# A hybrid decoder step on one Trainium2 core: two stages of a hand-written order change places

## What is computed

```python
h = _rmsnorm(x, g_norm1) * (1.0 + scale1) + shift1
z = h @ w_in                      # q|k|v|gates of both mixers
qk = jax.nn.silu(conv_b + sum(xpad[:, j:j + T] * conv_w[j] for j in range(4)))   # mixer A (mLSTM): 4-tap convolution of q and k
ha = _head_norm(_mlstm(...)) * jax.nn.sigmoid(o_a)
la = jax.nn.log_sigmoid(lr_b @ w_alpha + b_alpha) / 16                            # mixer B (GLA): log decay per channel and token
hb = _head_norm(_gla(qb, kb, vb, la, S0)) * jax.nn.silu(r_b)
y = (jax.nn.sigmoid(g_a) * ha + jax.nn.sigmoid(g_b) * hb) @ w_out
x = x + gate1 * y
x = x + gate2 * (silu(h2 @ w_ffn_gate) * (h2 @ w_ffn_up)) @ w_ffn_down
```

## Time and profile before

| | before |
|---|---|
| median of three runs | 1924.56 us |
| the profiled execution | 1924.94 us |
| its span, first to last instruction | 1923.1 us |
| PE (TensorE) busy | 98% |
| VectorE / ScalarE / GpSimd busy | 55% / 37% / 36% (DVE / ACT / POOL) |
| mean granted TensorE clock | 0.992 of full speed |

### The profile page before, as it was taken

One profiled execution on the slowest core, in us unless ns is written; L12 is line 12 of the kernel. 1 busy time (PEld: TensorE's weight loads), 2 busy tenths in 40 slices (PEclk: granted clock), 3 DMA queues, 4 the chain that ended last, 5 costly groups with the idle time before them and its releaser, 6 DMA issues.

```text
span 1923.1 us, 33344 instructions
## 1 busy us (share of the span) xinstructions
PE 1884.8 (98%) x13211; PEld 1805.1 (94%) x13211; DVE 1066.3 (55%) x1875; ACT 701.5 (36%) x1449; POOL 706.9 (37%) x600
## 2 busy tenths in 40 slices
PE   7899999999999999999999999999999999999998
PEld 4899999999999999999998899999999999999998
DVE  5740654414553236524174679886756675666566
ACT  4533434334233243342343554322232223222327
POOL 3221332212232213313132585433454345434544
PEclk8999999999999999999999999999999999999999
DMA  9241221332222322214233553111121112111212
GB/s 338 75 101 50 75 81 53 107 84 69 81 58 70 105 80 72 59 58 130 54 87 112 189 148 95 44 34 55 45 67 36 54 45 66 39 51 45 67 40 96
DMA packets 212226, 154.62 MB, mean 80 GB/s; under 512 B 11252, under 2 KB 196788, under 8 KB 211560
## 3 DMA queue, kind: packets, MB, share of 16 engines
q1 hardware_dynamic: 211770, 152.27, 26.7%
q10 hardware_dynamic: 302, 0.22, 0.0%
HBM read 130.96 MB, written 21.50 MB: 79 GB/s over the span
## 4 chain that ended last, share of the span: by engine, by line
PE 85%; DVE 7%; issue 2%; POOL 2%; ACT 2%; DMA 1%; SPq 0%; ACTq 0%; DVEq 0%; POOLq 0%
PE bank L923 36%; PE bank L2134 19%; PE bank L2103 12%; PE bank L1011 3%; PE bank L2001 2%; PE bank L1029 2%; PE bank L1031 1%; PE bank L1034 1%; PE bank L959 1%; PE bank L1968 1%; PE bank L1072 1%; PE bank L946 1%; DVE y_rows L2748 1%; PE bank L1061 1%; DVE y_rows L2567 1%
## 5 line engine op out<-in xcount | busy, mean ns | idle before, releaser
L1287 POOL TENSOR_TENSOR w_lo<-w_raw,w_hi 128x512 fp32r<-128x512 f32 x128 | 187.3, 1464 | 692.2 <-ACT w_hi L1094 692.2
L923 PE MATMUL bank<-h_hi,w_hi 128*128 128x352 f32 x1536 | 326.1, 334 | 1.4 <-ACT w_hi L1094 1.4
L923 PE MATMUL bank<-h_hi,w_lo 128*128 128x352 f32 x1536 | 311.5, 324 | 1.2 <-POOL w_lo L1287 1.1
L923 PE MATMUL bank<-h_lo,w_hi 128*128 128x352 f32 x1536 | 310.6, 324 | 0.0
L923 PEld LDWEIGHTS bank<-h_hi,w_hi 128*128 128x128 f32 x1536 | 255.2, 188 | 16.3 <-issue 12.1
L923 PEld LDWEIGHTS bank<-h_hi,w_lo 128*128 128x128 f32 x1536 | 258.3, 188 | 2.7 <-POOL w_lo L1287 2.7
L923 PEld LDWEIGHTS bank<-h_lo,w_hi 128*128 128x128 f32 x1536 | 258.3, 188 | 0.0
L2433 POOL TENSOR_TENSOR f_lo<-w_raw,f_hi 128x512 fp32r<-128x512 f32 x107 | 144.1, 1352 | 195.7 <-ACT f_hi L2198 195.7
L2433 POOL TENSOR_TENSOR w_lo<-w_raw,w_hi 128x512 fp32r<-128x512 f32 x107 | 144.1, 1352 | 152.4 <-ACT w_hi L2198 152.4
L2782 DVE SCALAR_TENSOR_TENSOR x_t<-bank,ada,x_t 128x352 f32<-128x352 f32 (+1 forms) x288 | 156.0, 567 | 54.8 <-PE bank L2103 38.4
L1094 ACT ACTIVATE w_hi<-w_raw 128x512 fp32r<-128x512 f32 x128 | 80.4, 628 | 153.9 <-PE bank L923 153.8
(11 more groups left out here) (506 smaller groups left out, 3898.3 us busy)
## 6 DMA issues: line engine op xcount, KB each, us to landing
w_raw<-in_w_in SPq DMA_DIRECT2D x128, 256.0 KB, 2.9
w_ada_tile<-in_w_ada SPq DMA_DIRECT2D x32, 512.0 KB, 4.3
w_raw<-in_w_out SPq DMA_DIRECT2D x48, 256.0 KB, 2.8
w_raw<-in_w_ffn_gate SPq DMA_DIRECT2D x44, 256.0 KB, 3.0
w_raw<-in_w_ffn_up SPq DMA_DIRECT2D x44, 256.0 KB, 2.9
w_raw<-in_w_ffn_down SPq DMA_DIRECT2D x44, 256.0 KB, 2.6
w_ada_ring<-in_w_ada SPq DMA_DIRECT2D x8, 1024.0 KB, 7.8
x_scratch<-x_turned_rows SPq DMA_DIRECT2D x1, 4224.0 KB, 14.0
```

The source lines that it names most:

```text
L923: last = pe.matmul(g.ps[b][:, 0:n], x[:, s, k, :], y[:, 4 * h + k, c0:c0 + n], start=(h == 0 and k == 0 and m == 0), stop=(h == 1 and k == ...
L1287: pool.tensor_tensor(Wl[:, s], raw[:, r], Wh[:, s].bitcast(F32), ALU.subtract).then_inc(s_lo, 1)
```

## The change

In "B", which stands for heads 0 to 2, the stages ("level5", 20) and ("conv_k", 20) change places. In "L", the last head, the stage level6_k goes from slot 8 to slot 7, so that it stands ahead of ada_load1 instead of behind it. Levels count from zero, so level5 is the sixth level and level6_k are the keys of the seventh. Nothing else is changed.

```diff
@@ -528,15 +528,15 @@
     "B": [("ada_load0", 3), ("conv_q", 7), ("taps_q", 8),
-          ("silu_q", 10), ("ada0", 14), ("level3", 14), ("ada_load1", 15), ("level4", 16), ("vt0", 16), ("conv_k", 20),
-          ("level5", 20), ("level6", 22), ("ada1", 22), ("taps_k", 24), ("level7", 26), ("adas0", 27), ("ada_load2", 27), ("vt1", 27),
+          ("silu_q", 10), ("ada0", 14), ("level3", 14), ("ada_load1", 15), ("level4", 16), ("vt0", 16), ("level5", 20),
+          ("conv_k", 20), ("level6", 22), ("ada1", 22), ("taps_k", 24), ("level7", 26), ("adas0", 27), ("ada_load2", 27), ("vt1", 27),
...
     "L": [("ada_load0", 2), ("level3", 2), ("level4", 4), ("ada0", 5), ("level5_k", 6),
-          ("level5", 6), ("gate_r0", 7), ("ada_load1", 8), ("level6_k", 8), ("level6", 8), ("level7", 10), ("ada1", 11),
+          ("level5", 6), ("gate_r0", 7), ("level6_k", 7), ("ada_load1", 8), ("level6", 8), ("level7", 10), ("ada1", 11),
```

## The result

| | before | after |
|---|---|---|
| median of 20 runs each | 1926.67 us | 1929.85 us |
| ratio, with 95% interval | | 1.0019 (1.0013 to 1.0025) |
| the profiled execution | 1924.94 us | 1930.53 us |
| its span | 1923.1 us | 1928.8 us |

The change makes the kernel slower by 0.19%, 2.5 to 4.8 us by the interval. The forecast was 1925.6 us in a range of 1923.0 to 1928.4, a step of +1.05 us; the measured median lies 1.4 us above the range. Two things together put it there. The kernel before came out at 1926.67 us over 20 runs where the first three had given 1924.56, and the step, 3.2 us, is about three times the one forecast.

What follows compares the result with a forecast made beforehand. TensorE, busy 98% of the span, was taken as the bound, so only its waits count. Median 1924.56 plus 1.05 us (+0.35 in each of three B windows, L part 0) gave 1925.6 us, range 1923.0 to 1928.4.

Steps and rivals of the forecast that it cites:

- What bounds the kernel, and the 3.15 us that could be won: TensorE, 98% busy, loses 1.05 us per B window waiting at levels 5 and 6; 3.15 us in three windows.
- The L part costs nothing: Last head: moving level6_k to slot 7 leaves every engine's stream and SP's queue order as they were; cost 0.
- The order on VectorE, the wait of 0.64 us that goes: B windows: q_decayed of level 5 is written before the convolution, so TensorE's 0.64 us wait at level 5 goes.
- The short copy waits for GpSimd: B windows, level 6: the 24-element copy L1350 waits until GpSimd's product ends, 0.84 us beyond its 0.18 us.
- Rival 1: B windows: the 24-element copy passes GpSimd without waiting; -0.16 us per window, -0.5 us in three, 1924.1 us; chance 0.27.
- The new wait of 1.40 us: B windows, level 6: TensorE, free at 548.69, starts the scores at 550.09, waiting 1.40 us for q_decayed.
- Net +0.35 us per window, +1.05 us in three: B windows: a new 1.40 us TensorE wait replaces 0.64 + 0.41 us, making the kernel 1.05 us slower.
- Rival 2: Level 6 of B windows: GpSimd falls on the whole convolution; +1.94 us per window, +5.8 us, 1930.4 us; chance 0.06.
- The base: Whole kernel: the starting time to which the forecast step was added, the median shown, 1924.56 us.
- "The same", 0.90: Whole kernel: chance 0.90 that the time stays within 0.2%, 3.85 us, of the kernel before.
- Rival 4: Whole kernel: the change does nothing measurable, 1924.6 us; chance 0.20.

Runs made afterwards that it cites:

- e1: Changed kernel with the convolution of k behind level 6 instead of in front of it in the three B windows; ratio to before 0.9985 (0.9975 to 0.9995).
- e5: Kernel before with only the L part of the change, level6_k at slot 7; ratio to before 0.9998 (0.9989 to 1.0007).
- e2: Changed kernel with the convolution's four short instructions left in front of level 5, only the two long ones behind; ratio to before 1.0032 (1.0019 to 1.0045).
- e3: Kernel before with q_decayed of level 6 written three times over in the B windows; ratio to before 1.0053 (1.0040 to 1.0067).
- e4: Kernel before with q_decayed of level 6 written twice in the B windows; ratio to before 1.0013 (1.0004 to 1.0022).
- e6: Changed kernel with ada1 one piece later, slot 23 instead of 22; ratio to before 1.0028 (1.0019 to 1.0036).
- e7: e1 with GpSimd's level 5 product in the L window ahead of w_lo, slot 5 instead of 6; ratio to before 0.9964 (0.9950 to 0.9977).
- c1: The changed kernel, unedited, timed and profiled once more; ratio to before 1.0035 (1.0021 to 1.0048).
- e8: Kernel before with the swap of level5 and conv_k in the B window of head 0 alone; ratio to before 1.0014 (1.0003 to 1.0025).
- e10: Kernel before with the swap of level5 and conv_k in the B window of head 2 alone; ratio to before 1.0003 (0.9991 to 1.0014).

## Why the prediction was wrong

- *What bounds the kernel, and the 3.15 us that could be won:* right. e1 removes both waits and gains 1.18 us per window instead of 1.05. TensorE's scores of a level take 1.89 us when they follow a piece directly and 2.00 behind a gap (changed kernel, 546.92 and 554.43), so an ended wait gives back 0.1 us more than its gap. For the same reason TensorE is free 0.08 us earlier in the changed kernel than I had it (552.92 less 4.31 is 548.61, for 548.69), so that the wait is 1.51 us and not 1.40 while the scores start only 0.03 us later than forecast. These scores then take 0.03 us more than before (2.00 for 1.97), which gives 0.41 us for 0.35.
- *The L part costs nothing:* right, e5.
- *The order on VectorE, the wait of 0.64 us that goes:* right, to hundredths.
- *The short copy waits for GpSimd:* right, 0.99 us against 0.18. The rule of the Trainium skill that I had weighed ("Advanced Engine Details and Errata", VectorE Performance Modes), that a two-port instruction of VectorE and one of GpSimd block each other, is borne out for this copy too. Rival 1, the copy that passes, was wrong. In e2, with the copy out of the way, L1355 waited for GpSimd as I had worked out for that rival (it ended 0.58 us behind the product), but what was saved went to a w_lo that was 0.5 us later; so e2 does not test that rival's -0.5 us.
- *The new wait of 1.40 us:* right in size, 1.51 us. *"Net +0.35 us per window, +1.05 us in three":* **this is the step that failed.** It prices a microsecond of TensorE's waiting at a microsecond. Measured in the windows of the profiled execution, the waits cost 1.2 us and the falls of the clock behind two of them 3.0 us. The new gap was put together from two shorter ones. In the trace of before, gaps of 0.47 and 0.25 us by the bracket have no fall behind them. It also held two longer cases, which I passed over: a wait of 1.77 us at level 5 in the L window with the clock at 1.00 behind it (e3, e4 and e6 show falls behind the same wait), and the waits of 1.21 and 1.11 us in the feed-forward phase with the fall at 1308.7 us behind them. So the record held a fall behind short waits, and the sum had no term for one.
- *Rival 2*, slower because GpSimd covers the whole convolution: its mechanism did not happen. L1355 and L1356 took 0.84 and 1.34 us.
- *The base:* I took the median of three runs, 1924.56 us, for the kernel's time. Twenty give 1926.67. With that base and the forecast step the time would have been 1927.7 us, inside the range, and with my base and the measured step (1924.56 + 3.18) also 1927.7: it took both errors to leave it.
- *"The same", 0.90:* it came out, at 0.19% against my bound of 0.2%, but for a reason I had not seen; that is luck. Rival 4, no effect, does not fit the interval, which excludes 1.

Shown: that lengthening the wait at level 6 alone, in the old order, brings falls (e3), that 0.75 us did not in three windows (e4), that without the wait there are none in six (e1, e7), nor in any of the 15 windows with waits of at most 0.75 us, and that a fall adds about 1.5 us to a window. Open: what chooses between the waits of the same length; no run was made to test it. In the profiles at hand 9 of 15 stretches with a wait of 1.31 to 1.51 us by the bracket at level 6 in kernels with all three windows touched had a fall (after, c1, e2, e3, e6), and 2 of 3 in e8 to e10; of the waits of 1.77 us in L, 3 of 12. Reading the kept traces again afterwards, I find one regularity. In each profile all changes of the granted clock lie on the marks of one regular beat. The 14 of these 30 waits with a fall behind them began between 0.13 of a beat ahead of a mark and 0.30 behind it, the 16 without between 0.39 and 0.79 behind it. So the moment seems to decide. It is not the whole rule: in e6 a wait of 1.52 us that began at 0.15, in the feed-forward phase at 1112.34, had no fall behind it.

## What to carry to other kernels

Two short waits of TensorE can be cheaper than one long one. Here 0.64 + 0.41 us cost their own length, while one wait of 1.5 us at level 6 cost its length and, in 11 of 18 cases, another 1.5 or 3.0 us through the clock behind it. At nearly the same sum there are only the three windows of e4: 0.47 and 0.75 us by the bracket, without a fall, against one wait of 1.34. Before a stage is moved ahead of another on a queue, look for the next deadline behind both: the convolution had to go behind level 6, where nothing waited for it, not between two levels that TensorE was due to ask for. And when a trace repeats a stretch several times, compare the lengths of its copies first; equal edits with unequal lengths are a reason to look at the granted clock.

## What the hardware showed that I had not expected

- The granted clock falls in portions. The missing clock of a fall was 1.70 to 1.71 us or 3.41 to 3.42 us in all the mixer's falls of this study, and the stretch grew by 1.5 or by 3.0 us.
- A copy of 24 elements on VectorE took 0.99 us beside GpSimd's TENSOR_TENSOR and 0.17 to 0.18 without it. GpSimd in turn took 1.76 us for a w_lo of 1.29 when VectorE's product ran beside it, and the delay of 0.5 us went on through the instructions that follow on three engines (e2).
